# Mixer 1: the low parts of the weights on VectorE alone, and the squares' sums at each stage's start within the fourth granule

## The reference, cut to what matters

```python
def rmsnorm(x, g):
    xf = x.astype(jnp.float32)
    y = xf * lax.rsqrt(jnp.mean(xf * xf, axis=-1, keepdims=True) + NORM_EPS)
    return (y * g.astype(jnp.float32)).astype(x.dtype)

def swiglu(x, w_gate, w_up, w_down):
    return (jax.nn.silu(x @ w_gate) * (x @ w_up)) @ w_down

for l in range(DEPTH):                      # first stack
    f = swiglu(rmsnorm(x, ffn1_pre_g[l]), ...)
    x = x + FFN_RESIDUAL_WEIGHT * rmsnorm(f, ffn1_post_g[l])
    m = token_mixing(rmsnorm(x, mix_pre_g[l]), w_in[l], ...)
    x = x + rmsnorm(m, mix_post_g[l])
    f = swiglu(rmsnorm(x, ffn2_pre_g[l]), ...)
    x = x + FFN_RESIDUAL_WEIGHT * rmsnorm(f, ffn2_post_g[l])
```

## Time and profile before

| | |
|---|---|
| time, median of 3 runs | 3469.97 us (3467.99 to 3471.78) |
| profiled execution, its time | 3471.96 us |
| profiled execution, its span | 3470.2 us |
| mean granted TensorE clock | 0.991 |
| PE busy | 3369.2 us, 97% of the span |
| DVE busy | 1756.2 us, 51% |
| ACT busy | 1414.8 us, 41% |
| POOL busy | 311.8 us, 9% |

### The profile page before, as it was taken

The page is one execution under the profiler, slowest core; times in us unless marked ns, Lnnn a source line. Parts: engine busy times, 40 slices in busy tenths (PEclk is TensorE's granted clock), DMA queues, the critical chain, the costliest instruction groups (busy, mean ns, idle before and its releaser), DMA issues.

```text
span 3470.2 us, 52759 instructions
## 1 busy us (share of the span) xinstructions
PE 3369.2 (97%) x21254; PEld 2937.3 (85%) x21254; DVE 1756.2 (51%) x2382; ACT 1414.8 (41%) x2394; POOL 311.8 (9%) x167
## 2 busy tenths in 40 slices
PE   8999999899999999999899999999999999999998
PEld 7887876788888888876788889879999988799998
DVE  5442556554425442556544426745665267366643
ACT  4322445432224322445433224465443344654432
POOL 0000122100000000122100002210000022100000
PEclk9999999999999999999999999999999999999999
DMA  4343321223332332311233332212222321122322
GB/s 116 96 120 102 101 61 55 61 85 96 88 101 87 95 97 88 107 55 55 61 89 92 94 100 68 55 47 73 91 91 90 101 60 53 53 72 88 95 87 86
DMA packets 330447, 287.45 MB, mean 83 GB/s; under 512 B 9666, under 2 KB 326170, under 8 KB 330294
## 3 DMA queue, kind: packets, MB, share of 16 engines
q1 hardware_dynamic: 329348, 283.90, 27.4%
q10 hardware_dynamic: 945, 1.37, 0.1%
HBM read 283.10 MB, written 5.27 MB: 83 GB/s over the span
## 4 chain that ended last, share of the span: by engine, by line
PE 86%; DVE 8%; ACT 4%; DMA 1%; issue 1%; SPq 0%; ACTq 0%; DVEq 0%
PE ps L605 22%; PE ps L606 21%; PE ps L607 21%; PE ps L651 3%; PE ps L652 3%; PE ps L653 3%; PE ps L1806 1%; PE ps L1808 1%; PE ps L1807 1%; DVE m_aconv L2249 1%; DVE y L780 1%; PE ps L1395 1%; PE ps L1419 1%; PE ps L1434 1%; DVE x L864 1%
## 5 line engine op out<-in xcount | busy, mean ns | idle before, releaser
L605 PE MATMUL ps<-xhi,whi 128*128 128x512 f32 (+2 forms) x3056 | 1057.0, 346 | 7.5 <-DVE m_aconv L2200 7.2
L606 PE MATMUL ps<-xlo,whi 128*128 128x512 f32 (+2 forms) x3056 | 1048.8, 343 | 0.0
L607 PE MATMUL ps<-xhi,wlo 128*128 128x512 f32 (+2 forms) x3056 | 1044.8, 342 | 0.0
L597 DVE TENSOR_TENSOR wlo<-raw,whi 128x1024 fp32r<-128x1024 f32 (+1 forms) x402 | 485.2, 1207 | 1099.4 <-ACT whi L590 1096.8
L590 ACT ACTIVATE whi<-raw 128x1024 fp32r<-128x1024 f32 (+1 forms) x493 | 513.2, 1041 | 1151.0 <-PE ps L607 1041.2
L605 PEld LDWEIGHTS ps<-xhi,whi 128*128 128x128 f32 x3056 | 578.4, 189 | 93.3 <-issue 17.3
L607 PEld LDWEIGHTS ps<-xhi,wlo 128*128 128x128 f32 x3056 | 577.2, 189 | 69.5
L606 PEld LDWEIGHTS ps<-xlo,whi 128*128 128x128 f32 x3056 | 577.9, 189 | 66.0 <-issue 0.5
L605 PE MATMUL ps<-hhi,whi 128*128 128x512 f32 (+2 forms) x1056 | 359.0, 340 | 1.9 <-issue 1.9
L606 PE MATMUL ps<-hlo,whi 128*128 128x512 f32 (+2 forms) x1056 | 358.0, 339 | 0.0
L607 PE MATMUL ps<-hhi,wlo 128*128 128x512 f32 (+2 forms) x1056 | 357.7, 339 | 0.0
(11 more groups left out here) (282 smaller groups left out, 5202.1 us busy)
## 6 DMA issues: line engine op xcount, KB each, us to landing
raw<-in_ffn_w_up_dram SPq DMA_DIRECT2D x176, 512.0 KB, 3.7
raw<-in_ffn_w_down_dram SPq DMA_DIRECT2D x120, 512.0 KB, 3.4
raw<-in_w_in_dram SPq DMA_DIRECT2D x94, 512.0 KB, 3.8
raw<-in_ffn_w_gate_dram SPq DMA_DIRECT2D x88, 512.0 KB, 3.7
raw<-in_w_out_dram SPq DMA_DIRECT2D x32, 512.0 KB, 3.4
raw<-in_ffn_w_down_dram SPq DMA_DIRECT2D x24, 256.0 KB, 2.7
tbias_scratch<-rev_scratch SPq DMA_DIRECT2D x1, 3072.0 KB
y<-tbias_scratch SPq DMA_DIRECT2D x6, 512.0 KB, 5.6
```

What stands on the lines that cost most here:

```text
L597: eng.tensor_tensor(lo[:, 0:n], raw[slot][:, 0:n], hi[:, 0:n].bitcast(F32), ALU.subtract).then_inc(b.s.weights_split, 1)
L605: pe.matmul(o, wh, hi[:, t0:t0 + w], start=first, stop=False)
L606: pe.matmul(o, wh, lo[:, t0:t0 + w], start=False, stop=False)
L607: ins = pe.matmul(o, wl, hi[:, t0:t0 + w], start=False, stop=last)
```

## The change

It does four things.

1. POOL no longer makes low parts in mixer 1 (23 a layer). DVE makes them: the fifth granule's (granule 4) behind the first three evacuations, and then that of granule g + 2 right behind the evacuation of granule g.
2. At every edge, DVE makes the fourth granule's low part between the two halves of the squares' sums (`fourth_lo`), where it made it after both halves (F stages) or POOL made it (mixers).
3. At every edge, PE's sum 0 moves from the middle of the third granule's second half to behind the whole third granule, and sum 1 from behind the third granule into the middle of the fourth: behind 24 of its 48 matmuls in an F stage, behind 4 of its 8 tiles in a mixer. In the second stack the sums go to unused columns of PSUM banks that the granules use (`spare`), as two matmuls of 132 columns instead of one of 264, and the third granule isn't cut any more: before, half of its tiles (`rest`) ran behind the norm's logarithm.
4. Mixer 1's first four steps have 8, 6, 5, 5 tiles of fill and not 6, 6, 6, 6. In the first one, PE runs four tiles, sum 1, four tiles, and then the scores.

```diff
@@ steps of mixer 1
-            steps[4 * p + i].tiles = tiles[6 * i:6 * i + 6]
+            n = ([0, 8, 14, 19, 24] if p == 0 else [0, 6, 12, 18, 24])[i:i + 2]
+            steps[4 * p + i].tiles = tiles[n[0]:n[1]]
...
+        def spare(g, h):
+
+            w = IN[g][h][1]
+            return ps[:, 2 * h:2 * h + 2, w:w + w // 2]
@@ pe_pre_sum
-            pe.matmul(ps[:, sum_bank(g, f"pre {h}"), 0:w], ones[:, 0:P], y[:, 0, c0:c0 + w],
-                      start=True, stop=True).then_inc(e.norm_sums, 1)
+            if KIND[g][1] == "1":
+                pe.matmul(ps[:, sum_bank(g, f"pre {h}"), 0:w], ones[:, 0:P], y[:, 0, c0:c0 + w],
+                          start=True, stop=True).then_inc(e.norm_sums, 1)
+                return
+            for i in range(2):
+                ins = pe.matmul(spare(g, h)[:, i, :], ones[:, 0:P], y[:, 0, c0 + i * (w // 2):c0 + (i + 1) * (w // 2)],
+                                start=True, stop=True)
+            ins.then_inc(e.norm_sums, 1)
@@ pe_first
                 for t in tiles[2][:half]:
                     tile(h, 2, t)
-                if h == 1:
-                    pe_pre_sum(pe, g, 0)
                 for t in tiles[2][half:]:
                     ins = tile(h, 2, t)
-                if h == 1:
-                    pe_pre_sum(pe, g, 1)
-            for h in range(2):
-                if rest:
-                    pe.wait_ge(e.norm_log, pre(g, h))
-                for t in rest:
-                    ins = tile(h, 2, t)
             ins.then_inc(b.s.granules_done, 1)
+            pe_pre_sum(pe, g, 0)
@@ DVE at an edge
-                for h in range(2):
-                    dve_x_sum(dve, g + 1, h, ch)
+                dve_x_sum(dve, g + 1, 0, ch)
+                fourth_lo(dve, g + 1)
+                dve_x_sum(dve, g + 1, 1, ch)
...
+        def fourth_lo(dve, g):
+            b = b1 if KIND[g][1] == "1" else b2
+            split_lo(dve, b, GB[KIND_AT[g]](LAYER[g]) + 3, 1, handover=(g == 0))
@@ F stages, PE and DVE
-            pe_first(pe, b, g, f.gb(l), tiles, rest)
-            pe_up_granule(pe, b, l, f, 0, 3)
+            pe_first(pe, b, g, f.gb(l), tiles)
+            pe_up_granule(pe, b, l, f, 0, 3, lambda: pe_pre_sum(pe, g, 1))
...
-            lo_split(0, 3)
             dve.wait_ge(e.norm_made, pre(g, 1))
@@ mixer 1, PE, DVE, POOL
                 if st.sc == 0:
-                    for part in st.parts:
-                        fill(part)
+                    fill(st.tiles[:4])
+                    pe_pre_sum(pe, sub, 1)
+                    fill(st.tiles[4:])
...
             evac(2)
+            split_lo(dve, b, mgb(l) + 4, 0)
...
                     if g < 24:
                         evac(g)
+                        split_lo(dve, b, mgb(l) + g + 2, g % 2)
...
-        def pool_mix1(pool, l):
-
-            for g in range(3, 26):
-                split_lo(pool, b1, mgb(l) + g, g % 2, handover=(g == 3))
@@ mixer 2, PE and POOL
-            pe.wait_ge(s.weights_split, g2b(l) + 3 + 1 + CR)
-            for h, (t0, w) in enumerate(halves(b)):
-                pe.wait_ge(e.norm_log, pre(sub, h))
+            for g in range(3, 8):
                 for t in range(8):
-                    ins = part_mm(pe, ps[:, gbank(3) + h, 0:w], whi[1][:, t * P:t * P + P], wlo[1][:, t * P:t * P + P],
-                                  xhi[:, t, t0:t0 + w], xlo[:, t, t0:t0 + w], t == 0, t == 7)
-            ins.then_inc(s.granules_done, 1)
-            for g in range(4, 8):
-                for t in range(8):
+                    if g == 3 and t == 4:
+                        pe_pre_sum(pe, sub, 1)
                     gtile(g, t)
...
-            for g in range(3, SPLIT2_DVE):
-                split_lo(pool, b2, g2b(l) + g, g % 2, n_of(g), handover=(g == 3))
+            for g in range(4, SPLIT2_DVE):
+                split_lo(pool, b2, g2b(l) + g, g % 2, n_of(g), handover=(g == 4))
```

More of the change, by code:

```diff
@@ L169, in schedule1 @@
     for st in steps:
-        st.parts = [st.tiles[0:2], st.tiles[2:4], st.tiles[4:6]]
+        st.parts = [st.tiles[0:2], st.tiles[2:4], st.tiles[4:]]
         st.done_in = [[g for g, t in part if t == 7] for part in st.parts]
@@ L638, in sum_bank @@
             n = {"post 1": 0, "pre 0": 1, "pre 1": 2}[what]
-            return {"F1": (1, 3, 1), "M1": (6, 4, 6), "M2": (6, 6, 7), "F2": (6, 6, 7), None: (4, 4, 4)}[
+            return {"F1": (1, 3, 1), "M1": (6, 4, 6), "M2": (1,), "F2": (1,), None: (4,)}[
                 KIND[g] if g < NSTAGES else None][n]
+        def spare(g, h):
+            w = IN[g][h][1]
+            return ps[:, 2 * h:2 * h + 2, w:w + w // 2]
         def ycols(g, h):
@@ L672, in pe_pre_sum, with pe_first @@
                 pe.wait_ge(e.norm_log, post(g - 1, 1))
-            pe.matmul(ps[:, sum_bank(g, f"pre {h}"), 0:w], ones[:, 0:P], y[:, 0, c0:c0 + w],
-                      start=True, stop=True).then_inc(e.norm_sums, 1)
-        def pe_first(pe, b, g, gb, tiles, rest=()):
+            if KIND[g][1] == "1":
[6 more added lines that the diff above has]
+            ins.then_inc(e.norm_sums, 1)
+        def pe_first(pe, b, g, gb, tiles):
             def view(bank, h, apart=False):
@@ L719, in pe_first @@
                     tile(h, 2, t)
-                if h == 1:
-                    pe_pre_sum(pe, g, 0)
                 for t in tiles[2][half:]:
                     ins = tile(h, 2, t)
-                if h == 1:
-                    pe_pre_sum(pe, g, 1)
-            for h in range(2):
-                if rest:
-                    pe.wait_ge(e.norm_log, pre(g, h))
-                for t in rest:
-                    ins = tile(h, 2, t)
             ins.then_inc(b.s.granules_done, 1)
+            pe_pre_sum(pe, g, 0)
         def act_norm(act, idx, bank, dst):
-            w = dst.shape[1]
             act.wait_ge(e.norm_sums, idx)
-            act.activation(dst, ps[:, bank, 0:w], ACT.Ln, bias=eps[:, :], scale=1.0 / D).then_inc(e.norm_log, 1)
+            src, log = (ps[:, bank, 0:dst.shape[1]], dst) if isinstance(bank, int) else (
+                bank, dst.rearrange("p (a t) -> p a t", a=2))
+            act.activation(log, src, ACT.Ln, bias=eps[:, :], scale=1.0 / D).then_inc(e.norm_log, 1)
             act.wait_ge(e.norm_log, idx)
@@ L747, in act_pre_norm @@
             t0, w = IN[g][h]
-            act_norm(act, pre(g, h), sum_bank(g, f"pre {h}"), r[:, t0:t0 + w])
+            act_norm(act, pre(g, h), sum_bank(g, f"pre {h}") if KIND[g][1] == "1" else spare(g, h), r[:, t0:t0 + w])
         def act_x_hi(act, g, col, h, p):
@@ L917, in sp_ffn, with pe_up_granule @@
                     load_raw(sp, b, f.gb(l) + UP_GRAN + 6 * m + q, q % 2, src, (k, PAIR))
-        def pe_up_granule(pe, b, l, f, i, q):
+        def pe_up_granule(pe, b, l, f, i, q, between=None):
             g = f.gb(l) + 4 * i + q
@@ L927, in pe_up_granule @@
             for o in range(2):
+                if o == 1 and between is not None:
+                    between()
                 for kk in range(4):
@@ L1008, in pe_ffn @@
                       for kk in range(4) for o in range(2)] for q in range(3)]
-            rest = []
-            if b.conv:
-                tiles[2], rest = tiles[2][0::2], tiles[2][1::2]
-            pe_first(pe, b, g, f.gb(l), tiles, rest)
-            pe_up_granule(pe, b, l, f, 0, 3)
+            pe_first(pe, b, g, f.gb(l), tiles)
+            pe_up_granule(pe, b, l, f, 0, 3, lambda: pe_pre_sum(pe, g, 1))
             with pe.Fori(1, UP_ITERS) as i:
@@ L1167, in lo_split @@
             def lo_split(i, q):
-                split_lo(dve, b, gb + 4 * i + q, q % 2, handover=(g == 0 and isinstance(i, int) and q == 3))
+                split_lo(dve, b, gb + 4 * i + q, q % 2)
             def conv(i, up):
@@ L1257, in dve_out @@
                 hi, lo = home(g, *divmod(j, nq))
-                split_lo(dve, b, gb + j, j % 2, qs[j % nq] * PAIR, handover=(qs is OUT_Q and j == 2), hi=hi, lo=lo)
+                split_lo(dve, b, gb + j, j % 2, qs[j % nq] * PAIR, hi=hi, lo=lo)
             if KIND[g][1] == "1" and g + 1 < NSTAGES and KIND[g + 1][1] == "2":
@@ L2478, in dve_setup @@
                             ps[:, 3, 0:PCOL[5] + PSIZE[5] - PSIZE[0]]).then_inc(s_pc, 1)
-            for h in range(2):
-                dve_x_sum(dve, 0, h, ch)
+            dve_x_sum(dve, 0, 0, ch)
+            fourth_lo(dve, 0)
+            dve_x_sum(dve, 0, 1, ch)
             dve.wait_ge(s_ld[3], 16)
@@ L2588, in _ @@
                 pool_y(pool, b1, l * 3)
-                pool_mix1(pool, l)
                 pool_y(pool, b1, l * 3 + 1)
```

## The result

| | before | changed |
|---|---|---|
| median | 3469.30 us (3467.99 to 3471.78, 4 runs) | 3501.72 us (3499.13 to 3503.13, 4 runs) |
| profiled execution, its span | 3470.2 us | 3497.4 us |
| mean granted clock of it | 0.991 | 0.988 |

The change makes the kernel slower: the ratio is 1.0092, 95% interval 1.0074 to 1.0109. The medians are 32.4 us apart, the two profiled spans 27.2 us (the profiled execution of the changed kernel was its fastest).

The account below looks back on a forecast made before the run. The prediction took PE as the bound, busy 3369.2 of 3470.2 us. Terms of 9.6, 6.1, 2.1 and 4.3 made 22.1; with 14.6 for the clock, +36.7 on the 3469.97 median gave 3507 us, range 3488 to 3520.

Parts of the forecast that it names:

- Shift and clock together: Whole kernel: later sum 1 delays PE's next stops and the clock falls behind new waits; 3500 to 3515 us, chance 0.65.
- F1 edges: Four feed-forward edges, including the first stage: later sum 1 delays the fifth granule's low part, PE idles 3.2 us; +9.6 us.
- F2 edges: The other two feed-forward edges: sum 1 3.1 us later, PE resumes 3.0 late after 5.8 us of idle; +6.1 us.
- M2 edges: Two mixer 2 edges: the wait removed at sum 1 reappears at the evacuation behind the norm; +2.1 us.
- M1: Mixer 1, both layers: 1.7 us an edge, a low part delaying logits and transposes, and 0.45 a layer elsewhere; +4.3 us.
- The clock: Behind eight new waits in feed-forward stages and mixer 1, the granted clock falls to 0.50; +14.6 us.
- The +0.7 a layer for two later units: Rest of mixer 1: two units whose exponentials are behind a low part cost 0.7 us a layer.
- pure gain: All edges: 9.4 us of idle before the sums goes and nothing later takes it up; 3461 us, chance 0.05.
- Gain and shift cancel: Feed-forward lateness below the removed waits, mixer 1 at its lower bound, no clock loss; within 7 us of 3470, chance 0.05.
- Shift without clock: The delay terms stand, but PE idles just short of what lowers the clock; +22, 3492 us, chance 0.12.
- Mixer 1 worse: Mixer 1: low parts waiting for ACT block logits or transposes in more steps; 10 us more, 3517 us, chance 0.13.

Follow-up runs that it names:

- experiment 1: Changed kernel with sum 1 back right behind sum 0 and the fourth low part behind both x_sums in the six feed-forward stages: 3482.3 us, ratio 1.0036.
- experiment 2: Changed kernel, sum 1 still late, with the fifth granule's high and low parts ahead of the norms in the feed-forward stages: 3475.2 us, ratio 1.0017.
- experiment 5: Changed kernel; mixer 2's fifth and sixth granules wait only for their own banks' evacuation, the fifth's high part goes between the norms: 3482.9 us, ratio 1.0036.
- experiment 3: Changed kernel with mixer 1's low part of granule 5 behind the second unit's logits on DVE: 3495.8 us, ratio 1.0075.
- experiment 7: Changed kernel with unread matmuls filling PE's gap behind the fourth granule of each feed-forward stage: 3495.1 us, ratio 1.0073.
- experiment 6: Changed kernel: split before norms in five feed-forward stages, first stage as before the change, granule 5's low part behind logits, mixer 2 waiting for own banks: 3442.5 us.
- experiment 4: Changed kernel with mixer 1's low parts from granule 4 on made by GpSimd again: 3496.4 us, ratio 1.0075.
- experiment 9: The kernel of experiment 6 with mixer 1's low parts from granule 4 on by GpSimd: 3442.9 us, ratio 0.9922.

## Why the prediction was right, point by point

The forecast was 3507 (3488 to 3520), the time is 3501.7. Shift and clock together were the likeliest case, and it is the one that came. The sizes are less exact than the total looks: the sum was +36.7 (22.1 and 14.6 of clock), the profiled executions show +27.2 (17.1 and 10.1). F1, F2 and M2 are within 0.4 us of their forecasts; M1 and the clock came out 4.0 and 4.5 us below theirs. That the medians are 32.4 us apart, and so nearer, is luck as far as the terms go.

- **F1 edges**: 9.6 forecast; growth without the clock 1.9, 2.4, 2.6 and 2.4, 9.3 together. The chain's 6.23 us came as 6.2, the idle of 3.2 as 2.94 (3.17 in the first stage). Experiments 1 and 2 show the cause from both sides. The first stage's edge was 2.9 late, near the 2.7 reckoned (46.67 against 43.76), but 1.05 of it was taken up at 270.17, where a wait that the profile puts down to issue went from 1.89 to 0.84.
- **F2 edges**: 6.1 forecast, 2.8 + 2.9, together 5.8 measured; the idle of 5.8 came as 5.58 and 5.51. Size and mechanism are right.
- **M2 edges**: 2.1 forecast, 0.7 + 1.0 = 1.7 measured, and the wait is 6.5 where it was to be near 7. That the removed wait only reappears at the next stop is right; experiment 5 shows that this stop was needless.
- **M1**: 4.3 forecast for both layers, 0.3 + 0.0 = 0.3 measured. This is, beside the clock, the term that was mis-sized. The second unit's transposes came 2.4 us later in the stage in both layers, where 3.1 was reckoned; behind them the mixer gave back 0.7 and 0.9 us where 0.45 each was to be lost (an estimate, with the 1.4 for the two tiles taken as forecast). The wait of 4.0 at the second unit's transposes came as 3.16, with 0.43 more for granule 4's low part ahead of it. The low part of granule 5 ran at 424.24; less the 1.86 us by which the stage began later, 422.4, where 422.9 was forecast. Place and releaser are as predicted, and experiment 3 shows that this low part is the cause. The +0.7 a layer for two later units isn't seen: the wait of 0.47 at 519.94 is 0.44 now, and the one for L1649's line fell from 4.48 to 3.98, by 0.5 where 0.3 was forecast.
- **The clock**: 14.6 forecast, 10.1 in the profiled executions. Of the four F1 edges only two lowered it: two of the three with 2.94 us of idle, and not the first stage's with 3.17. The four F1 edges therefore lost 3.3 us where 6.0 was forecast, the two F2 edges 3.7 for 4.6, M1 grew by 4.2 for 4.0, and M2, forecast at nothing, fell by 1.0. The reading that 2.79 us is near the shortest wait behind which it falls was wrong: in the kernel before it also fell behind two waits of 2.08 and 2.09 us and one of 1.54 (see the last section). Experiment 7 shows the price apart.
- **The rivals**: *pure gain* (3461) is ruled out by the result itself. Its condition, the fifth granule's split ahead of the norm, is what removed the F stages' loss in experiment 2; with the other edits of experiment 6 the change became a gain. *Gain and shift cancel* did not come. *Shift without clock* did not come, though in two stages it did. *Mixer 1 worse* did not come: DVE's order hurt at the one place that was counted.

On the shared interface, the Trainium skill (GPSIMD Engine Reference, 8. Key points) says that GpSimd contends with VectorE's instructions that have two SBUF inputs or run in a 2-port perf mode. The traces agree for two inputs: with POOL making no low part in mixer 1, the longest L1640 falls from 2.60 to 0.43 us. L1629, with one tensor as input, was stretched as much (2.66 us beside a low part on POOL that took 2.4); whether it ran in such a mode no trace here shows. The 55 us of VectorE time show in no time of the kernel, as experiments 4 and 9 say.

## What to carry to other kernels

A wait in front of an instruction says what is late now; before you move the instruction back to hide it, follow what it releases, through every queue, to the bottleneck engine's next stop. If something independent (here the next weights' split) stands in an in-order queue behind that chain, move it ahead first; then the same change gains where it lost. And on TensorE count an idle gap at more than its length: in the changed kernel the clock fell behind 14 of the 16 waits of 2.77 us and more that follow the start, and each fall cost 1.5 to 3.1 us of PE's working time.

## What the runs showed of the hardware

Two gaps of the same length and releaser ended differently in the changed kernel. Behind 2.94 us of idle at 717.89 the clock was 0.56 (the row under experiment 7); behind 2.94 us at 1094.49 it stayed at full rate:

```profile
1094.49:1097.49 3.00, 3.00 (x13) 2.46 (x14) 2.21 (x3) 0.00 (x0) 0.00 (x0) 1.00 0.61 174
```

Nor is it the place that decides. Experiments 3, 4 and 5 left the F1 stages as they are in the changed kernel, and at this same edge, again behind 2.94 us, the clock stayed at 1.00 in the trace of experiment 3 and fell in those of 4 and 5. That of experiment 4:

```profile
1092.83:1096.30 3.47, 3.47 (x8) 2.77 (x9) 2.21 (x3) 0.00 (x0) 0.00 (x0) 0.51 0.68 193
```

Shorter waits aren't safe either. In the kernel before, in mixer 2, a wait of 2.09 us and then the window behind it:

```profile
2180.55 0.36 PE L1806 MATMUL ps<-xhi,whi 128*128 128x264 f32 x1 [2.09 <-DVE m_vt L2218]
2181.95:2185.30 3.35, 3.35 (x16) 1.93 (x14) 3.00 (x3) 0.84 (x3) 1.68 (x1) 0.50 0.13 22
```

At 3021.61 in that trace it fell behind a wait of 1.54 us. The same wait of 2.09 us was followed by no fall in experiments 5 and 9. So between 2.1 and 3.2 us the length of a wait alone doesn't tell whether the clock falls, and executions of the same code differ by it: in experiment 5 the six stages ahead of mixer 2 took 3.6 us more than in the changed kernel, with 3.6 us more lost to the clock. The four executions of the changed kernel have spans of 3497.4 to 3501.4 us at mean clocks of 0.988 and 0.987; 0.001 of clock is 3.5 us of such a span, so the clock could set them apart, but only one of them was profiled.
